# Routing weights side by side, the second half of x turned early, memory loaded by column halves

## The reference

```python
def first_block(x, mem, ...):
    ...
    m = rms_norm(mem, mem_norm_g[l])
    x = x + memory_cross_attention(hc, m, cross_w_q[l], cross_w_kv[l], ...)   # kv = m @ w_kv
    hm = rms_norm(x, moe_norm_g[l])
    x = x + hierarchical_moe(hm, router_w_group[l], router_b_group[l], router_w_expert[l], ...)

def hierarchical_moe(h, w_group, b_group, w_expert, b_expert, w_gate, w_up, w_down):
    g_logits = hr @ w_group                       # 4 groups
    g_sel = argmax(g_logits + b_group)
    e_all = hr @ w_expert                         # 32 experts, 8 of each group
    ...
```

## Time and profile before

| | |
|---|---|
| Time, median of 3 runs | 982.11 us (981.62 to 982.72) |
| Profiled execution | 981.87 us, span 980.1 us, mean granted clock 0.984 |
| PE busy | 947.4 us, 97% of the span |
| PEld busy | 818.1 us, 83% |
| DVE busy | 741.0 us, 76% |
| ACT busy | 622.1 us, 63% |
| HBM read | 213.03 MB, 218 GB/s over the span |

### The profile page before, as it was taken

The page is one execution under the profiler, slowest core; times in us unless marked ns, Lnnn a source line. Parts: engine busy times, 40 slices in busy tenths (PEclk is TensorE's granted clock), DMA queues, the critical chain, the costliest instruction groups (busy, mean ns, idle before and its releaser), DMA issues.

```text
span 980.1 us, 13833 instructions
## 1 busy us (share of the span) xinstructions
PE 947.4 (97%) x5035; PEld 818.1 (83%) x5035; DVE 741.0 (76%) x1083; ACT 622.1 (63%) x949; POOL 20.5 (2%) x40
## 2 busy tenths in 40 slices
PE   6999999989899999999999799999999999999996
PEld 5888888878788888888888699999997788888875
DVE  4567686467699999999999778888797555555575
ACT  4786684565387878877877856656565543444455
POOL 7000000000000000000000000000000000000000
PEclk9999999999799999999999999999999999999999
DMA  9655426225279999999999255637366555565531
GB/s 323 204 167 194 160 87 215 86 87 210 92 276 376 349 368 377 361 357 363 359 370 343 66 175 168 226 128 256 118 220 220 182 191 185 180 205 171 189 111 43
DMA packets 102379, 214.64 MB, mean 219 GB/s; under 512 B 5613, under 2 KB 60161, under 8 KB 96705
## 3 DMA queue, kind: packets, MB, share of 16 engines
q1 hardware_dynamic: 100784, 211.83, 61.4%
q0 software_dynamic: 1392, 2.20, 0.8%
q10 hardware_dynamic: 160, 0.07, 0.0%
HBM read 213.03 MB, written 1.05 MB: 218 GB/s over the span
## 4 chain that ended last, share of the span: by engine, by line
PE 89%; DVE 6%; ACT 3%; issue 1%; DMA 0%; SPq 0%; DVEq 0%; ACTq 0%
PE bank L2092 22%; PE bank L2094 22%; PE bank L2093 21%; PE bank L2626 5%; PE bank L2627 5%; PE bank L2628 5%; PE bank L2097 4%; DVE w_lo L435 1%; DVE w_lo L437 1%; DVE xT_lo L1443 1%; PE bank L2413 1%; DMA xs<-in_mem_dram 0%; PE bank L2414 0%; PE bank L2639 0%; PE bank L2640 0%
## 5 line engine op out<-in xcount | busy, mean ns | idle before, releaser
L2092 PE MATMUL bank<-w_hi,xT_hi 128*128 128x512 f32 (+1 forms) x704 | 280.6, 399 | 4.8 <-DVE w_lo L437 3.2
L2094 PE MATMUL bank<-w_hi,xT_lo 128*128 128x512 f32 (+1 forms) x704 | 275.0, 391 | 0.0
L2093 PE MATMUL bank<-w_lo,xT_hi 128*128 128x512 f32 (+1 forms) x704 | 274.6, 390 | 0.0
L2092 PEld LDWEIGHTS bank<-w_hi,xT_hi 128*128 128x128 f32 x704 | 133.0, 189 | 32.7 <-DVE w_lo L437 5.4
L2094 PEld LDWEIGHTS bank<-w_hi,xT_lo 128*128 128x128 f32 x704 | 132.6, 188 | 27.8
L2093 PEld LDWEIGHTS bank<-w_lo,xT_hi 128*128 128x128 f32 x704 | 132.8, 189 | 25.4
L435 DVE TENSOR_TENSOR w_lo<-stage,w_hi 128x1024 fp32r<-128x1024 f32 (+3 forms) x102 | 117.0, 1147 | 40.2 <-ACT w_hi L421 39.3
L421 ACT ACTIVATE w_hi<-stage 128x1024 fp32r<-128x1024 f32 (+3 forms) x103 | 102.9, 999 | 40.9 <-PE bank L2628 18.7
L2626 PE MATMUL bank<-xT_hi,w_hi 128*128 128x256 f32 x448 | 127.0, 283 | 0.0
L2627 PE MATMUL bank<-xT_lo,w_hi 128*128 128x256 f32 x448 | 126.8, 283 | 0.0
L2628 PE MATMUL bank<-xT_hi,w_lo 128*128 128x256 f32 x448 | 126.8, 283 | 0.0
(11 more groups left out here) (401 smaller groups left out, 1368.3 us busy)
## 6 DMA issues: line engine op xcount, KB each, us to landing
stage<-in_w_in_dram SPq DMA_DIRECT2D x36, 1024.0 KB, 5.0
stage<-in_w_gate_up_dram SPq DMA_DIRECT2D x44, 512.0 KB, 4.5
more<-in_expert_w_down_dram SPq DMA_DIRECT2D x17, 1024.0 KB, 6.8
stage<-in_expert_w_gate_dram SPq DMA_DIRECT2D x33, 512.0 KB, 5.8
stage<-in_expert_w_up_dram SPq DMA_DIRECT2D x33, 512.0 KB, 6.7
more<-in_expert_w_gate_dram SPq DMA_DIRECT2D x31, 512.0 KB, 5.6
more<-in_expert_w_up_dram SPq DMA_DIRECT2D x31, 512.0 KB, 6.5
stage<-in_expert_w_down_dram SPq DMA_DIRECT2D x15, 1024.0 KB, 7.0
```

Of the source, the lines that this page charges most:

```text
L2092: mm(o, k_hi, v_hi, start=start, stop=False)
L2093: mm(o, k_hi, v_lo, start=False, stop=False)
L2094: return mm(o, k_lo, v_hi, start=False, stop=stop)
```

## The change

Memory is loaded by halves of its columns, and between them the two halves of unit 0; unit 2 comes ahead of x, and POOL's small loads wait for x. Memory's first two banks are turned when its first column half is there. ACT and DVE take bank 0, the first half of unit 0, bank 1, the second half, and then banks 2 and 3; PE starts unit 0's products on the first half (`first_lo`). The squares and the norm of memory move behind unit 1. In the router the high and low weights stand side by side (`r_parts`), so that the high part of x meets both in one product of 72 columns and the low part meets the high weights in one of 36; DVE adds the two sums first. The second half of x is turned between the second and third block of the first half's products, in banks 4 and 7 instead of 4 and 5, and DVE adds the second half of x after bank 0's low part. Some semaphore signals that nobody waits for are dropped.

```diff
@@ -134,8 +134,8 @@
-    r_hi = sb("r_hi", [P, KD, CHOICES], F32R)
-    r_lo = sb("r_lo", [P, KD, CHOICES], F32R)
+    r_parts = sb("r_parts", [P, KD, 2, CHOICES], F32R)
+    r_hi, r_lo = r_parts[:, :, 0], r_parts[:, :, 1]
...
@@ -459,7 +460,7 @@
-                + ["catc0", "catc1", "co10", "co11", "catc2", "catc3", ("moe0", 4), ("moe1", 5), ("router", 6), ("moe2", 4), ("moe3", 5), ("rank", 7)]
+                + ["catc0", "catc1", "co10", "co11", "catc2", "catc3", ("moe0", 4), ("moe1", 5), ("router", 6), ("moe2", 4), ("moe3", 7), ("rank", 7)]
...
@@ -652,15 +653,20 @@
 
         def choose_group():
             b = product(dve, "router")
+            both = b[:, 0:T * 2 * CHOICES].rearrange("p (t w n) -> p w t n", t=T, w=2)
+            then(nc.vector.tensor_copy(biased[:], both[:, 1]))
+            ins = tt(logits[:], both[:, 0], biased[:], ALU.add)
+            frees(ins, "router")
+            been_read(dve, "router")
             for t in range(T):
-                ins = stt(biased[:, t], b[:, CHOICES * t:CHOICES * t + CHOICES], rstd[:, t:t + 1], r_bias[:], ALU.mult, ALU.add)
+                ins = stt(biased[:, t], logits[:, t], rstd[:, t:t + 1], r_bias[:], ALU.mult, ALU.add)
             then(ins)
             first_of_largest(scratch(2, GROUPS), biased[:, :, 0:GROUPS], best, GROUPS,
                              hot[:].rearrange("p (t g) -> p t g", t=T)).then_inc(sem("group_chosen"), 1)
             dve.wait_ge(sem("group_chosen"), 1)
             for t in range(T):
-                ins = ts(logits[:, t], b[:, CHOICES * t:CHOICES * t + CHOICES], rstd[:, t:t + 1], None, ALU.mult)
-            frees(ins, "router")
+                ins = ts(logits[:, t], logits[:, t], rstd[:, t:t + 1], None, ALU.mult)
+            then(ins)
 
         def place_tokens():
             b = product(dve, "rank")
...
@@ -730,12 +735,15 @@
 
     @block.sync
     def _(sp):
-        for t in range(T):
-            sp.dma_start(xs[:, t], a["mem"][0, P * t:P * t + P]).then_inc(sem(f"mem_loaded{t}"), 16)
-        load_unit(sp, *before[0], 0)
+        for c in range(2):
+            at = slice(512 * c, 512 * c + 512)
+            sp.dma_start(xs[:, :, at], a["mem"][0].rearrange("(t p) d -> p t d", p=P)[:, :, at]).then_inc(sem(f"mem_loaded{c}"), 16)
+            sp.dma_start(stage[:, 0, 1024 * c:1024 * c + 1024].rearrange("p (k n) -> p k n", k=2),
+                         before[0][0][:, 2 * c:2 * c + 2]).then_inc((main.up_landed if c else main.landed)[0], 16)
         load_unit(sp, *before[1], 1)
+        load_unit(sp, *before[2], 2)
         sp.dma_start(x[:], a["x"][0].rearrange("(t p) d -> p t d", p=P)).then_inc(sem("x_loaded"), 16)
-        for u in range(2, U_MOE):
+        for u in range(3, U_MOE):
             load_unit(sp, *before[u], u)
 
         def swiglu_loads(both_of, down_of, base, steps, st=main, before_steps=None):
...
@@ -819,7 +827,7 @@
     @block.gpsimd
     def _(pool):
         nc.gpsimd.memset(one_col[:], 1.0).then_inc(sem("ones_set"), 1)
-        pool.wait_ge(sem("mem_loaded1"), 16)
+        pool.wait_ge(sem("x_loaded"), 16)
         for dst, src in small_loads:
             pool.dma_start(dst, src).then_inc(sem("constants_loaded"), 16)
 
...
@@ -917,14 +925,20 @@
 
         act.wait_ge(sem("ones_set"), 1)
         warm_up(ACT.Sqrt)
-        squares(xs, k_cross, [("mem_loaded0", 16)])
         frees(copy_to(norm_g[:, MEM_G], "mem_gain"), "mem_gain")
         been_read(act, "mem_gain")
+        high_parts("mem", MEM_G, (0,))
+        act.wait_ge(main.landed[0], 16)
+        nc.scalar.activation(w_hi[:, 0, 0:1024], stage[:, 0, 0:1024], ACT.Copy).then_inc(main.half_ready, 1)
+        high_parts("mem", MEM_G, (1,))
+        act.wait_ge(main.up_landed[0], 16)
+        nc.scalar.activation(w_hi[:, 0, 1024:SLOT], stage[:, 0, 1024:SLOT], ACT.Copy).then_inc(main.hi_ready, 1)
+        split[0] = 1
+        high_parts("mem", MEM_G, (2, 3))
+        splits_to(2)
+        squares(xs, k_cross, [("mem_loaded0", 16), ("mem_loaded1", 16)])
+        splits_to(3)
         roots("mem")
-        high_parts("mem", MEM_G, range(2))
-        splits_to(1)
-        high_parts("mem", MEM_G, range(2, 4))
-        splits_to(2)
 
         def tables():
             act.wait_ge(sem("constants_loaded"), 16 * len(small_loads))
...
@@ -1153,10 +1167,9 @@
         high_parts("moe", MOE_G, (0, 1))
         act.wait_ge(sem("x_cross"), 2)
         chunk_squares(1).then_inc(sem("norm_sums"), 1)
+        high_parts("moe", MOE_G, (2, 3))
+        roots("moe")
         raw_high(1, 0)
-        high_parts("moe", MOE_G, (2,))
-        roots("moe")
-        high_parts("moe", MOE_G, (3,))
         raw_high(1, 1)
         warm_up(ACT.Exp)
         act.wait_ge(sem("route_diffs"), 1)
...
@@ -1489,13 +1502,19 @@
         tmp_a, tmp_b = silu_t[:].rearrange("p t f -> p (t f)"), silu_g[:].rearrange("p t f -> p (t f)")
 
 
-        stats(xs, k_cross, [("mem_loaded1", 16)], "mem")
         been_read(dve, "mem_gain")
-        low_parts("mem", MEM_G, range(2))
-        splits_to(1)
-        low_parts("mem", MEM_G, range(2, 4))
+        low_parts("mem", MEM_G, (0,))
+        dve.wait_ge(main.half_ready, 1)
+        tt(w_lo[:, 0, 0:1024], stage[:, 0, 0:1024], w_hi[:, 0, 0:1024].bitcast(F32), ALU.subtract).then_inc(sem("first_lo"), 1)
+        low_parts("mem", MEM_G, (1,))
+        dve.wait_ge(main.hi_ready, 1)
+        tt(w_lo[:, 0, 1024:SLOT], stage[:, 0, 1024:SLOT], w_hi[:, 0, 1024:SLOT].bitcast(F32), ALU.subtract).then_inc(main.lo_ready, 1)
+        split[0] = 1
+        low_parts("mem", MEM_G, (2, 3))
+        splits_to(2)
+        stats(xs, k_cross, [("mem_loaded0", 16), ("mem_loaded1", 16)], "mem")
+        splits_to(3)
         halves("mem")
-        splits_to(2)
 
         splits_to(6)
         inverse_of(head_inv[:, 0:8], head_sums[:, 0:8], CROSS, "row_sums", nth(ROW_SUMS, "kc"), "row_inverse")
...
@@ -1752,13 +1771,15 @@
 
         raw_low(0)
         chunk_squares(0)
-        low_parts("moe", MOE_G, (0, 1))
+        low_parts("moe", MOE_G, (0,))
         add_chunk(1, C_CO, U_CO + 3, "x_cross")
+        low_parts("moe", MOE_G, (1,))
         chunk_squares(1)
+        low_parts("moe", MOE_G, (2,))
         dve.wait_ge(sem("norm_sums"), nth(NORMS, "moe"))
         then(tt(sums[:], x_sums[:, :, 0], x_sums[:, :, 1], ALU.add))
         inverse_of(inverse[:], sums[:], D, "norm_sums", nth(NORMS, "moe"), "norm_inverse")
-        low_parts("moe", MOE_G, (2, 3))
+        low_parts("moe", MOE_G, (3,))
         dve.wait_ge(sem("norm_rstd"), nth(NORMS, "moe"))
         choose_group, place_tokens, choose_experts, between = routing(dve, then)
         choose_group()
...
@@ -2105,8 +2126,13 @@
         def wide_unit(u, c, h, cols, th, tl, xt=None, last=None, before={}):
 
             s = u % RING
-            pe.wait_ge(lo_ready, u + 1)
+            if u in main.halved:
+                pe.wait_ge(sem("first_lo"), 1)
+            else:
+                pe.wait_ge(lo_ready, u + 1)
             for k in range(4):
+                if k == 2 and u in main.halved:
+                    pe.wait_ge(lo_ready, u + 1)
                 if k == 3 and last is not None:
                     last()
                 if k in before:
...
@@ -2155,7 +2181,8 @@
         pe.wait_ge(sem("first_loaded"), 16 * len(first_loads))
         b = to_fill(pe, "mem_gain")
         fills(nc.tensor.transpose(b[:, 0:KD], mem_gain_in, ident[0:KD, 0:KD]), "mem_gain")
-        turn("mem", xs, [("mem_loaded0", 16), ("mem_loaded1", 16)])
+        for c in range(2):
+            turn("mem", xs, [(f"mem_loaded{c}", 16)], (2 * c, 2 * c + 1))
         for c in range(4):
             if c < 3:
                 wide(C_K + c, 2 * c, xt="mem")
...
@@ -2379,18 +2406,21 @@
 
         pe.wait_ge(sem("router_lo"), 2)
         for half in range(2):
-            if half:
-                turn("moe", x, [("x_cross", 2)], (2, 3))
             if half == 0:
                 b = to_fill(pe, "router")
-                mm(b[:, 0:T * CHOICES], before_it[:], zeros[:, 0:T * CHOICES], start=True, stop=False)
+                mm(b[:, 0:T * 2 * CHOICES], before_it[:], zeros[:], start=True, stop=False)
             for k in range(4 * half, 4 * half + 4):
+                if k == 2:
+                    turn("moe", x, [("x_cross", 2)], (2, 3))
                 if k % 2 == 0:
                     been_read(pe, f"moe{k // 2}")
                 kk = at_k("moe", k)
                 for t in range(T):
-                    ins = three(b[:, CHOICES * t:CHOICES * t + CHOICES], xT_hi[:, kk, P * t:P * t + P], xT_lo[:, kk, P * t:P * t + P],
-                                r_hi[:, k], r_lo[:, k], start=False, stop=k == KD - 1 and t == T - 1)
+                    at = 2 * CHOICES * t
+                    mm(b[:, at:at + 2 * CHOICES], xT_hi[:, kk, P * t:P * t + P], r_parts[:, k].rearrange("p w n -> p (w n)"),
+                       start=False, stop=False)
+                    ins = mm(b[:, at:at + CHOICES], xT_lo[:, kk, P * t:P * t + P], r_hi[:, k],
```

(1 more changed line is left out.)

16 lines of the change are left out of this document (8 added, 8 removed).

## The result

The changed kernel takes 976.15 us (median of 4 runs, 975.19 to 976.59), beside 982.41 for the kernel before (4 runs, 981.62 to 982.96): ratio 0.9936, 95% interval 0.9918 to 0.9953, so 6.3 us faster. The forecast was 973.0 and its range ended at 975.9. The profiled execution took 975.19 (span 973.4) beside 981.87, 6.7 less.

The account below looks back on a forecast made before the run. PE, 89% of the chain, was taken to bound the kernel, plus its few waits for other engines. Start 4.8 plus routing 4.2 gives 9.0 off 981.87: 972.9, given as 973.0 us, range 970.3 to 975.9.

Parts of the forecast that it names:

- The start's term, 4.8: Start of the kernel: unit 1 starts 4.9 or 3.5 us earlier than 20.20; 4.8 us taken.
- a wait at the constants: Sign of being wrong: DVE waits for late small loads, expected at 38.8 us, needed at 39.2, cover 0.7 us.
- a wait for a low part: Sign of being wrong: PE waits for DVE's low part of the weights before unit 1 or 2.
- a longer stretch of low clock behind the routing: Sign of being wrong: PE's clock stays low behind the routing for longer than before.
- the first product near 9.3: Expected sign at the start: PE's first product of unit 0 at about 9.3 us, not 12.82.
- unit 1 near 15.3: Expected sign at the start: unit 1 begins near 15.3 us, when its low part is ready.
- The landings: Start loads: halves of memory and unit 0 alternate, landing at 4.6, 5.9, 7.2, 8.5 us, at 400 GB/s.
- the vanished gap: Start: only 0.3 us between last transpose and first product, instead of 3.2, taken to speak for full clock and 4.8.
- The end 3.5: Start's lower end: unit 0 loses the same 1.9 us to low clock, ends at 16.7; gain 3.5 us.
- the rival of double cost: Routing: wide products cost 0.21 us at full clock, only the early turn counts, 2 us; 975.1 us; 5%.
- start gained only in part: Rival: late constants, low clock in unit 0, or unit 2's low part late; gain 6.1, 975.8 us; 15%.
- halves land one after the other: Rival: each 512 KB transfer pays its own latency, first products 3 us later, start worth 1.5; 976.2 us; 3%.

Follow-up runs that it names:

- e1: The kernel before with only the routing part of the change; 978.97 us, ratio 0.9970 to the kernel before.
- e2: The kernel before with only the start part (halved loads, moved norm, POOL's wait); 978.54 us, ratio 0.9965 to the kernel before.
- e7: The changed kernel with dummy products keeping PE busy while it would wait for memory (nine before the first transposes, six between the turns); 975.48 us.
- e3: The changed kernel with both column halves of memory loaded ahead of both halves of unit 0; 974.74 us.
- e12: The changed kernel with both memory halves loaded first and products on constants in PE's waits around the routing; 975.72 us.
- e6: The changed kernel with POOL's small loads issued once memory's second half has landed, as before the change; 976.77 us.
- e5: The changed kernel with the 16 wide routing products split again into 32 narrow ones; 978.12 us.
- e9: The changed kernel with the turn of x's second half put back ahead of the router's fifth k instead of the third; 979.08 us.
- e11: The changed kernel with products on constants put into PE's waits around the routing; 975.18 us.
- e4: The changed kernel with memory loaded ahead of unit 0, by blocks of 128 tokens (4 KB rows), PE waiting for both; 976.13 us.
- e8: The changed kernel with both memory halves loaded first and nine dummy products ahead of the first transposes; 976.21 us.
- e10: The changed kernel with memory in 4 KB rows, its blocks alternating with unit 0's halves, PE waiting for both blocks; 977.12 us.

## Why the prediction was wrong

**The start's term, 4.8, is the step that failed: two of its inputs, the landing times and the clock of unit 0, were wrong.** The forecast was 4.8 + 4.2; the pair of traces gives 2.95 + 4.05. The traces put the whole miss on the start, and that is sharper than the evidence: by the medians of e1 and e2 the start is worth 3.7 and the routing 3.3, the latter under the forecast's lower end of 3.7. Before's start took 1.0 us longer in e1's trace and its routing 1.1 less in e2's, with the same code, so that 4.05 beside 4.2 is in part luck. Of the signs of being wrong that the prediction named (a wait at the constants, a wait for a low part, a longer stretch of low clock behind the routing) none came; what failed is what it expected to see, the first product near 9.3 and unit 1 near 15.3.

1. *The landings* (4.6, 5.9, 7.2, 8.5 us) were worked out with 400 GB/s from 5 to 13 us of before, where one source follows the other in long runs. In alternation 264 came from 3 to 6 us. Both second halves were 1.3 to 1.4 late, DVE's second half of unit 0 started at 10.97, and unit 1's low part was ready at 16.05 instead of 15.3. This is 0.75 us, or 1.0 by e7.
2. *The clock.* "I take 4.8, the end that the vanished gap speaks for" was the weak choice. The gap did vanish: the first product follows the last transpose without a pause, and it still ran at the half speed that the transposes showed. So the rule that I took from before, low clock behind 3.2 us without a product, does not decide it; e3 and e12, with the same code and waits of 1.57 and 1.38, start unit 0 at full and at half clock. PE also paused for 1.27 between the two turns, where the forecast had 0.1; whether that pause kept the clock low no run shows. Half clock for seven products is 0.75 to 1.0 us by e7. The end 3.5, which I had worked out for half clock with a first product at 9.3, is what came, less the 0.86 by which that product was late and with seven products at half clock instead of nine. The sum also set the end of unit 0 before (20.20) against a start (15.3); start against start it would have been 4.7 at most.
3. *The first product* was late by 0.86 (10.16 for 9.3), by the in-order PE: the second turn stands ahead of it in the code and waits for the second half (8.54 + 1.97, less the overlap at the end). The high and low parts of bank 0 and the first half of the weights were ready by 9.56. With PE at half clock this delay goes into the end of unit 0.
4. *What was to cost nothing did.* Norm behind unit 1, unit 2, the constants: no wait stands there. The cover at the constants was small again: the last positions, asked for at 34.6, landed 5.9 later, 0.6 us before DVE reads them at 41.09. That it held is in part luck, since x and with it POOL came 1.8 us later than forecast and DVE asked 1.9 later. In e6, with the old place of POOL's loads, unit 6 starts 1.1 later.
5. *The routing.* 4.05 beside 4.2. Products of 72 columns cost as those of 36 (0.11, 0.21), so the rival of double cost is out. The Trainium skill (TensorE: Matmul & The Clock Gate, Back-to-back issue gap) has 25 ns for up to 64 columns, which would have made the 16 products worth 0.4 us. The section gives that figure for a product by itself and says that it comes out too low where each has a load of its own, as here; the traces have 0.11 apart at full clock, 1.8 us for 16, and e5's median gives 2.0. The early turn leaves a wait of 0.67 where e2 has 1.41 and e9 has 1.47, and by e9 it also fills one of 0.91.
6. *The rival* "start gained only in part", 975.8, is what happened, but of its three reasons only the low clock in unit 0 was real. The late transfers stood in no rival: "halves land one after the other" had them 3 us late by a latency for each, and found 976.2 by the wrong road.

**The spread.** Five kernels have the changed kernel's start (it, e5, e6, e9, e11): their transposes of `arena` start between 43.85 and 45.49. The same routing code (it, e3, e4, e7, e8, e10) takes 10.83 to 12.13 from first product to gather. Most of these differences are where the clock falls and rises in one execution (in e9 the memory also landed 0.6 later, its second turn starting at 9.10 beside 8.54). In the kernels that spread most, the slow runs have the lower mean granted clock: e12 0.986 at 979.18 and 0.992 at 974.30, e9 0.984 at 979.77 and 0.989 at 977.22. In e1 it is the other way (0.989 at 980.51, 0.987 at 978.23), so that this mean, whose row reads 1.00 beside half speed at the start, does not explain every spread. A single trace is therefore good to about 1.5 us here, more than some terms of my sum; the 5 or 6 runs of one kernel spread over 0.2 to 4.9 us. The division of the start's miss between clock and data comes from one trace each; e7's median (0.7 under) fits it but is not clear of the spread.
